# Sample outputs of the SSD stage as three products of rounded halves, and two buffers of decay rows in place of three

## The reference

```
state = decay * state + B^T (x * dt)      # 128 x 512, an output of the kernel
y     = C state + d_skip * x              # one row of 512
```

## Time and profile before

| | us |
|---|---|
| median of 3 runs | 2538.93 (2535.07 to 2542.4) |
| the profiled execution: its time | 2538.79 |
| the profiled execution: its span | 2537.0 |
| SSD stage, about | 66 to 380 |

### The profile page before, as it was taken

The page is one execution under the profiler, slowest core; times in us unless marked ns, Lnnn a source line. Parts: engine busy times, 40 slices in busy tenths (PEclk is TensorE's granted clock), DMA queues, the critical chain, the costliest instruction groups (busy, mean ns, idle before and its releaser), DMA issues.

```text
span 2537.0 us, 27837 instructions
## 1 busy us (share of the span) xinstructions
PE 2118.4 (83%) x9848; PEld 1396.0 (55%) x9848; DVE 1466.1 (58%) x3149; ACT 975.0 (38%) x2482; POOL 684.3 (27%) x676
## 2 busy tenths in 40 slices
PE   5799879988989999987998899887777777777776
PEld 4777648765979989986544444432222222222222
DVE  4577782222464445524666666666677666666654
ACT  2456544222454444412333333333334333333333
POOL 0110221111020011001443444345444434344331
PEclk7899898998999999998999999999999999999999
DMA  2455442222446535535999999999999999999996
GB/s 71 125 162 175 145 148 86 92 94 88 143 133 184 157 109 166 169 142 218 422 421 421 421 418 412 421 414 421 421 421 421 421 421 421 421 421 421 422 421 250
DMA packets 209854, 714.20 MB, mean 282 GB/s; under 512 B 18530, under 2 KB 114370, under 8 KB 141491
## 3 DMA queue, kind: packets, MB, share of 16 engines
q0 software_dynamic: 74880, 545.29, 51.8%
q1 hardware_dynamic: 134834, 167.13, 20.9%
HBM read 691.32 MB, written 20.98 MB: 281 GB/s over the span
## 4 chain that ended last, share of the span: by engine, by line
DMA 34%; PE 14%; DVE 3%; ACT 2%; issue 1%; POOL 0%; ACTq 0%; POOLq 0%
DMA p_rows<-in_experts,p_idx 34%; PE bank L2041 10%; PE bank L2001 4%; DVE p_rows L1896 2%; ACT p_diag L1948 1%; ACT p_weight L1941 1%; POOL p_rows L1763 0%; PE bank L2011 0%; ACT p_gel L1938 0%; DVE p_x1b L1875 0%; ACT L1960 0%; ACT p_sc L1927 0%; ACT p_q L1920 0%; DVE p_x1b L1866 0%; ACT L1938 0%
## 5 line engine op out<-in xcount | busy, mean ns | idle before, releaser
L2041 PE MATMUL bank<-p_rows,p_diag 128*128 128x512 f32 (+1 forms) x1664 | 775.8, 612 | 199.2 <-ACT p_diag L1948 199.0
L1896 DVE CUSTOM_DVE_ANT_0 p_rows<-p_rows,p_hnb 128x1024 f32<-128x1024 f32 x416 | 510.0, 1226 | 359.3 <-DMA p_rows<-in_experts,p_idx 359.2
L1763 POOL DMA_INDIRECT p_rows<-in_experts,p_idx x416 | 441.6, 1062 | 836.5 <-PE bank L2041 579.2
L2041 PEld LDWEIGHTS bank<-p_rows,p_diag 128*128 128x128 f32 (+1 forms) x1664 | 306.9, 192 | 649.6 <-issue 326.2
L144 DVE TENSOR_TENSOR w_lo<-raw_w,w_hi 128x1024 fp32r<-128x1024 f32 x176 | 219.7, 1249 | 275.5 <-ACT w_hi L136 275.4
L1938 ACT ACTIVATE p_gel<-p_hid 128x2 f32<-128x2 f32 x260 | 52.9, 203 | 826.6 <-DVE p_hid L1896 822.6
L150 PE MATMUL bank<-x_hi,w_hi 128*128 128x264 f32 (+2 forms) x1152 | 347.5, 302 | 24.2 <-DVE w_lo L144 19.2
L151 PE MATMUL bank<-x_lo,w_hi 128*128 128x264 f32 (+2 forms) x1152 | 335.8, 292 | 0.0
L152 PE MATMUL bank<-x_hi,w_lo 128*128 128x264 f32 (+2 forms) x1152 | 334.8, 291 | 0.0
L150 PEld LDWEIGHTS bank<-x_hi,w_hi 128*128 128x128 f32 x1152 | 225.8, 196 | 40.1 <-DVE w_lo L144 18.2
L136 ACT CAST w_hi<-raw_w 128x1024 fp32r<-128x1024 f32 x176 | 183.6, 1044 | 157.8 <-PE bank L152 108.1
(11 more groups left out here) (358 smaller groups left out, 2993.8 us busy)
## 6 DMA issues: line engine op xcount, KB each, us to landing
raw_w<-in_w_merge SPq DMA_DIRECT2D x80, 512.0 KB, 3.6
raw_w<-in_w_z SPq DMA_DIRECT2D x32, 512.0 KB, 4.2
raw_w<-in_w_ssd SPq DMA_DIRECT2D x24, 512.0 KB, 7.0
s_sst<-in_state_ssd SPq DMA_DIRECT2D x16, 512.0 KB, 5.7
s_mix<-arow_kept SPq DMA_DIRECT2D x16, 512.0 KB, 5.3
s_sxb<-sx_kept SPq DMA_DIRECT2D x32, 256.0 KB, 3.8
o_sssd<-s_sst SPq DMA_DIRECT2D x16, 512.0 KB, 5.0
raw_w<-in_w_gla SPq DMA_DIRECT2D x16, 512.0 KB, 7.4
```

The costliest lines, as they stand in the source:

```text
L1763: nc.gpsimd.indirect_dma_start(row_of(row), None, k.dram["experts"], bass.IndirectOffsetOnAxis(idx[:, slot:slot + 1], 0)).then_inc(row_her ...
L1896: nc.vector.tensor_tensor_reduce(out=u, in0=u, in1=hn, scale=1.0, scalar=0.0, op0=ALU.mult, op1=ALU.add, accum_out=hid[:, n % 2, s:s + 1]) ...
L2041: last = nc.tensor.matmul(ps[b][0:width, :], diag[:, slot % DIAGS, 0:width], row_of(row)[:, D + half * 512:D + half * 512 + 512], start=s ...
```

## The change

The product in `sread` becomes three products of float32r halves (`three`). The masked C is rounded into `cmh` and its rest put into `cml`, once for each group, by two more VectorE instructions of 128 x 64 in `sprep`. Each new state is rounded into `sth` by a ScalarE copy of 128 x 512 in `samp`, and its rest put into `stl` by a GpSimd subtraction of 128 x 512 in `samp`; both have two buffers. ScalarE's copy waits for VectorE's L756 (`sst_done`) and, for the buffer, for TensorE's read of two samples before (`sst_read`). GpSimd waits for ScalarE, and TensorE for GpSimd.

`mix` has two buffers in place of three, and the decay rows are loaded one chunk ahead in place of two; `sxdt` lies in `yoff`, and VectorE waits for the write of `sxdt` to memory before it first writes `yoff` in a group; the unrounded masked C lies in a half of `xdt`.

```diff
-    MIXES, SPREADS = 3, 2
+    MIXES, SPREADS = 2, 2
...
-        cmask = sb("cmask", [P, NSAMP, NSAMP])
+        cmh, cml = sb("cmask_hi", [P, NSAMP, NSAMP], F32R), sb("cmask_lo", [P, NSAMP, NSAMP], F32R)
+
+        sth, stl = sb("sst_hi", [P, 2, GW], F32R), sb("sst_lo", [P, 2, GW], F32R)
...
-        sxdt = sb("sxdt", [NSAMP, GW])
+
+        sxdt = yoff[0:NSAMP, :]
...
-                    rows(g * TILES + i + 1)
+                    rows(g * TILES + i + MIXES - 2)
...
-                        pe.wait_ge(cmask_done, g + 1)
+                        pe.wait_ge(cmask_done, 2 * g + 2)
...
-                    pe.wait_ge(sst_done, g * NSAMP + i + 1)
-                    last = nc.tensor.matmul(ps[SY][0:NSAMP, :], cmask[:, i, :], sst[:, i, :], start=i == 0, stop=i == NSAMP - 1)
-                    last.then_inc(sst_read, 1)
+                    pe.wait_ge(sst_rest, g * NSAMP + i + 1)
+                    three(nc, ps[SY][0:NSAMP, :], (cmh[:, i, :], cml[:, i, :]), (sth[:, i % 2, :], stl[:, i % 2, :]), i == 0, i == NSAMP - 1).then_inc(sst_read, 1)
...
+                elif kind == "samp":
+                    q = g * NSAMP + i
+                    act.wait_ge(sst_done, q + 1)
+                    if q >= 2:
+                        act.wait_ge(sst_read, q - 1)
+                    nc.scalar.copy(sth[:, i % 2, :], sst[:, i, :]).then_inc(sst_round, 1)
...
+                    if i == 1:
+                        dve.wait_ge(sx_out, 16 * (g + 1))
...
-                    nc.vector.tensor_tensor(cmask[:, :, :], k.eye8[:, :, :], sxc[:, g % 2, C_TILE, :].unsqueeze(1).to_broadcast([P, NSAMP, NSAMP]),
+                    whole = xdt[:, g * STEPS % 2, 0:NSAMP * NSAMP].rearrange("p (a b) -> p a b", a=NSAMP)
+                    nc.vector.tensor_tensor(whole, k.eye8[:, :, :], sxc[:, g % 2, C_TILE, :].unsqueeze(1).to_broadcast([P, NSAMP, NSAMP]),
                                             ALU.mult).then_inc(cmask_done, 1)
+                    dve.wait_ge(cmask_done, 2 * g + 1)
+                    k.vlink(dve, nc.vector.tensor_copy(cmh[:, :, :], whole))
+                    nc.vector.tensor_tensor(cml[:, :, :], whole, cmh[:, :, :], ALU.subtract).then_inc(cmask_done, 1)
...
+                elif kind == "samp":
+                    q = g * NSAMP + i
+                    pool.wait_ge(sst_round, q + 1)
+                    nc.gpsimd.tensor_tensor(stl[:, i % 2, :], sst[:, i, :], sth[:, i % 2, :], ALU.subtract).then_inc(sst_rest, 1)
```

## The result

The changed kernel took 2560.17 us (median of 5 runs, 2558.15 to 2565.55); the kernel before, run beside it, 2539.5 us (5 runs, 2535.07 to 2544.58). The ratio is 1.0083, with a 95% interval of 1.0066 to 1.0100: slower. The profiled execution of after took 2560.59 us with a span of 2558.7 us, 21.7 us more than before's span. All of it arises in the SSD stage: VectorE's first instruction behind that stage, the clearing of `sso`, starts at 402.02 us where it started at 380.34 us.

The account below looks back on a forecast made before the run. In the SSD stage, TensorE's and VectorE's loops are almost equally long, with ScalarE between them. Terms of 7.2 + 2.8 + 2.0 + 2.7 + 1.0 = 15.7 us on 2538.8 gave 2554 us, range 2543 to 2564.

Parts of the forecast that it names:

- ScalarE's copies in steps 2 to 4: First three groups: copies queued behind VectorE's update delay weight rounding and PSUM copies; 7.2 us (steps 2, 3), 2.8 (step 4).
- The masked C: Two more VectorE instructions and two waits lie on the path while TensorE idles: 0.5 us in four groups, 2.0 us.
- TensorE's products: Sample reads save 0.19 us each, 6 us over 32, but TensorE then waits longer for L720: counted as nothing.
- The clock: Step 4's longer gap lowers TensorE's clock, 0 to 2.7 us per group; one in three at full price, 2.7 us.
- The rival of a clock that falls in every step 4: TensorE's clock falls at all three second tiles, 8.1 us, giving 2560 to 2566 us; chance 0.20.
- GpSimd's subtractions: At 1.04 us each they can slow VectorE's two-operand instructions, 0 to 8 us; medians say rare, 1 us.
- Wrong it would be ... if the last group's steps grew: Sign against the forecast: longer steps in the last group, which has no tiles; no size given.
- upper bound of 8 us: Most that GpSimd's subtractions could cost by slowing VectorE in steps 2 to 4 and the last group.
- the stage would end near 395 us: Sign for the forecast: the SSD stage ends near 395 us in place of 380.
- Decay rows: Loaded one chunk ahead they have 12 us, or some 8 in the last group, against 4.0 us landing: nothing.
- The rival in which the copies are hidden: ScalarE's idle 2.50 us hides the copies, TensorE sets the pace: 2535 to 2538.4 us, not slower; chance 0.18.

Follow-up runs that it names:

- no_rest: The changed kernel without GpSimd's subtractions, the rounded state multiplied in place of the rest: 2552.53 us, ratio 1.0069.
- first_no_rest: The changed kernel with the next tile's weights rounded ahead of ScalarE's sample copies and without GpSimd's subtractions: 2539.64 us, ratio 1.0005.
- round_first: The changed kernel with ScalarE rounding the next tile's weights ahead of a step's two sample copies: 2556.18 us, ratio 1.0082.
- wait_only: The kernel before with ScalarE waiting, at the place of the copies, for VectorE's sample updates, without any copy: 2548.44 us, ratio 1.0037.
- gp_only: The kernel before with two decay row buffers and a GpSimd subtraction behind each state update, which TensorE's read awaits: 2546.92 us, ratio 1.0040.
- two_mix: The kernel before with two buffers of decay rows in place of three, loaded one chunk ahead: 2535.83 us, ratio 1.0001.
- rest_late: As round_first, with GpSimd's subtractions held until VectorE ends the next tile's convolution steps: 2572.72 us, ratio 1.0140.

## Why the prediction was right, and which step of it was not

The forecast was 2554 us, slower; it came out slower, at 2560 us, inside the range. The queue on ScalarE was foreseen step by step; the size of GpSimd's term was not. That the total is only 6 us off is in part luck: by the account above the terms came to 26.3 us, and 4.6 us that no term foresaw came back at the stage's start and in the passages. Without them the kernel would stand near 2565 us, just past the range's end of 2564.

- **ScalarE's copies in steps 2 to 4 (7.2 + 2.8 us).** Right, also in its small parts: no_rest shows L144 waiting 1.63 us (1.7 was named), L700 0.33 us (0.3) and a step of 13.33 us (13.35). In its first group, where TensorE's clock stayed at 1.00, the three intervals and the second tile together are 3.1 us longer than before, 9.4 us for three groups, where 10.0 us was forecast. first_no_rest shows the cause is the order: with the rounding ahead of the copies the steps are 12.38 us and the kernel is not slower than before by more than the runs can tell.
- **The masked C (2.0 us).** Right, 2.3 us: 0.4 us in each of three groups, and 1.1 us in the last, where the cast met GpSimd's decay.
- **TensorE's products (nothing).** Right, a read is 0.72 us and L583 waits 1.93 us for what it saved and more.
- **The clock (2.7 us).** The forecast paid for one fall in three. In after all three second tiles ran partly at 0.50, at 1.5 us each (7.55 us in place of 6.05): 4.5 us. The rival of a clock that falls in every step 4 had the number of falls right, at too high a price for each (2.7). In round_first and first_no_rest, where the gap is 1.23 to 1.28 us, the products take 6.04 or 6.05 us and the intervals are back at 7.5 to 8.3 us. Over all the traces, 18 second tiles had a gap of 0.49 to 1.28 us ahead of them and none was slowed; 18 had one of 2.08 to 3.75 us, and 15 of them took 7.3 to 8.6 us. One in three was too few. GpSimd lengthened two of the gaps of after to 3.75 us, but in wait_only, without GpSimd's subtraction, 2.48 us went with three falls too. The term left out the last group, whose steps GpSimd lengthens and where the clock fell as well.
- **GpSimd's subtractions (1.0 us).** This is the step that failed, by its size. It read: "The medians say it is rare: 1 us." The medians were those of instructions that seldom met GpSimd's decays. The new subtractions are released by ScalarE's copy of a result that VectorE has just written, so they come at the same place in every step, and VectorE's next instructions there have two SBUF operands: L144 in the steps with tiles, L732 and L734 in the last group. The price of one subtraction was low too: 1.04 us, from the decay, where it takes 1.26 us at the least. In after, by line, busy us and mean ns, and for GpSimd the least, median and greatest ns:

```profile
L144 DVE TENSOR_TENSOR w_lo<-raw_w,w_hi 128x1024 fp32r<-128x1024 f32 x18 | 32.1, 1786 | 27.8 <-ACT w_hi L136 27.8
...
L732 DVE TENSOR_TENSOR s_state<-s_state,cdec 128x512 f32<-128x512 f32 x16 | 14.2, 890 | 0.0
L734 DVE TENSOR_TENSOR y<-y,s_yoff 128x512 f32<-128x512 f32 x16 | 13.0, 812 | 0.6
...
L799 POOL TENSOR_TENSOR s_sst_lo<-s_sst,s_sst_hi x32: 1262/1277/1735, 124.8 to 395.8; 128x512 fp32r<-128x512 f32 x32
```

  By the medians, after is 7.6 us above no_rest; by the ratios, each beside its own runs of before, 3.6 us, with intervals that overlap; in the traces the stage ends 6.7 us later. So the term measured some 4 to 8 us and not 1.0. That GpSimd costs time at all is sharper elsewhere: the ratio of gp_only to before is 1.0040 [1.0028, 1.0052], and round_first takes 16.5 us more than first_no_rest. By place, after has 6.4 us more than no_rest in the last group, 3.6 us in the nine steps and 1.7 us in the second tiles, and its start and passages are 4.9 us shorter. "Wrong it would be ... if the last group's steps grew": they grew, and gp_only shows that GpSimd alone does that. By its own sign of being wrong the forecast failed there. Its upper bound of 8 us held by the medians, and L144, L721 and L723 were rightly named as at risk; it was the choice between the ends that was bad. That the stage would end near 395 us is what no_rest shows (395.30); GpSimd makes it 402.02.
- **Decay rows (nothing).** Right (two_mix, 1.0001).
- **The rival in which the copies are hidden.** It doesn't hold for the change. It does describe first_no_rest, where they are hidden; and even there the shorter reads gain nothing, since the steps are then 12.38 us, above the 12.17 us that TensorE needed.

What stays open: how much of the shorter start and passages, 4.6 us in after, is the change's own. The start is as short or shorter in two_mix (99.29), and its kernel took no less time. The kernels with three row buffers reach that point at 101.82 to 103.65 us and those with two at 99.29 to 101.58, so the profiled execution of before lies at one end, and part of the 3.2 us may be its own.

No version found beats the kernel before. In the versions tried the rest is formed by GpSimd, which takes VectorE's time, or by VectorE itself, and the three short products save TensorE only 0.37 us of a step (two reads of 0.72 in place of 0.905 us).

## What to carry over

Where an instruction is added to an engine's queue, ask what is queued behind its wait: here the wait alone cost 9.7 us in the trace, 4.4 of them by TensorE's clock that fell in the longer gaps, and rounding the weights first took away nearly all of what the wait and the copies cost (first_no_rest). Work given to GpSimd is not free beside VectorE: look for what VectorE does in the microsecond after the release, because a subtraction that is released by way of VectorE's own result meets the same instruction each time, and an average over the kernel says nothing about it. Two causes that hide behind each other must be taken out together before either shows its price.

## What the runs showed of the hardware

An operation of VectorE with two SBUF operands and a two-operand subtraction of GpSimd took turns, whole instruction by whole instruction: 0.68 became 1.44 and 1.65 us, three convolution steps of 2.38 became 3.43, L144 of 1.22 became 2.02, and GpSimd's two subtractions took 2.95 and 3.43 us where they took 2.50 us when neither waited (in gp_only 3.46 in place of twice 1.04). Each ended by its own time, less 0.1 to 0.2 us, behind the end of the instruction that it waited for. An operation that read PSUM kept its 0.68 us beside them (L731, L733, L696). The cast of 64 columns, with one SBUF operand, was held as well: 0.92 us in place of 0.20. Work moved from GpSimd to VectorE made the steps shorter, 12.57 in place of 13.43 us.

GpSimd's subtraction of 128 x 512 took 1.26 us at the least with one float32r operand (after, rest_late), and 1.04 us where both operands were float32 (gp_only, which reads one tensor twice, and the decay). Whether the type does that was not tested.

TensorE's granted clock fell from 1.00 to 0.50 around 15 of 18 gaps of 2.08 to 3.75 us ahead of a second tile, and around none of 18 gaps of 0.49 to 1.28 us; 2.95 us went with a fall and 2.99 us without one (no_rest). A fall made the tile's 48 products take 7.3 to 8.6 us in place of 6.05.
